# A decoder trunk on one core: x's second token tile is transposed inside the first weight chunk of the feature-form products

## The reference

```python
for i in range(DEPTH):                      # DEPTH = 2
    h = rms_norm(x, norm_mix_g[i])
    x = x + (moba_mixer(h, ...) if i == 0 else retention_mixer(h, ...))
    x = x + sqrelu_mlp(rms_norm(x, norm_mlp_g[i]), mlp_w1[i], mlp_w2[i])

def sqrelu_mlp(h, w1, w2):                  # w1 1024 x 4096, w2 4096 x 1024
    return jnp.square(jax.nn.relu(h @ w1)) @ w2
```

## Time and profile before

| | |
|---|---|
| median of 3 runs | 675.47 us (673.47 to 677.33) |
| the profiled execution | 677.14 us |
| its span, first to last instruction | 675.4 us |
| mean granted clock of TensorE in it | 0.995 |
| PE busy | 664.5 us, 98% |
| PEld busy | 559.1 us, 83% |
| DVE busy | 424.0 us, 63% |
| ACT busy | 330.9 us, 49% |
| POOL busy | 25.7 us, 4% |
| read from HBM | 121.52 MB, 181 GB/s over the span |

### The profile page before, as it was taken

How to read it: one execution, slowest core, us unless ns; L and a number is a source line. 1 busy time by engine, 2 the same in 40 slices (tenths; PEclk the granted TensorE clock), 3 DMA queues, 4 the chain that set the end, 5 groups by cost and what they waited for, 6 DMA issues and landing times.

```text
span 675.4 us, 8900 instructions
## 1 busy us (share of the span) xinstructions
PE 664.5 (98%) x3296; PEld 559.1 (83%) x3296; DVE 424.0 (63%) x466; ACT 330.9 (49%) x432; POOL 25.7 (4%) x35
## 2 busy tenths in 40 slices
PE   7998999999999999999999999999999999999998
PEld 5877888888888888888888888888888888888887
DVE  5877766777777444557985656554468777744441
ACT  6575764655555333436445554543365555533320
POOL 0341200000000000000000000000000000000000
PEclk7999999999999999999999999999999999999999
DMA  8954537476555655553666445536648665555600
GB/s 310 390 199 146 175 113 263 137 205 186 183 186 186 212 200 202 180 196 126 193 195 201 161 129 183 185 125 186 195 119 248 187 186 186 186 187 194 211 1 31
DMA packets 82077, 122.98 MB, mean 182 GB/s; under 512 B 2176, under 2 KB 43904, under 8 KB 82048
## 3 DMA queue, kind: packets, MB, share of 16 engines
q1 hardware_dynamic: 81472, 121.05, 55.0%
q0 software_dynamic: 288, 1.31, 0.5%
q10 hardware_dynamic: 288, 0.21, 0.1%
HBM read 121.52 MB, written 1.05 MB: 181 GB/s over the span
## 4 chain that ended last, share of the span: by engine, by line
PE 88%; issue 3%; DVE 3%; POOL 1%; ACT 1%; DMA 1%; SPq 1%; DVEq 0%; POOLq 0%; ACTq 0%
PE acc L552 22%; PE acc L483 17%; PE acc L485 17%; PE acc L484 17%; PE acc L555 11%; DVE lo L972 1%; DMA rope_in<-in_rope_in 1%; SPq L369 1%; ACT hi L737 1%; POOL rope_g L424 1%; PE scr L485 1%; PE scr L484 1%; PE scr L483 1%; PE scr L682 1%; PE scr L623 1%
## 5 line engine op out<-in xcount | busy, mean ns | idle before, releaser
L972 DVE TENSOR_TENSOR lo<-raw,hi 128x2048 fp32r<-128x2048 f32 x109 | 249.4, 2290 | 119.9 <-ACT hi L737 117.9
L737 ACT ACTIVATE hi<-raw 128x2048 fp32r<-128x2048 f32 x109 | 209.0, 1918 | 131.6 <-PE acc L485 128.6
L552 PE MATMUL acc<-h_both,hi 128*128 128x512 f32 x640 | 224.0, 396 | 0.0
L555 PE MATMUL acc<-h_both,lo 128*128 128x256 f32 x640 | 178.3, 279 | 0.0
L552 PEld LDWEIGHTS acc<-h_both,hi 128*128 128x128 f32 x640 | 120.1, 188 | 28.5
L555 PEld LDWEIGHTS acc<-h_both,lo 128*128 128x128 f32 x640 | 120.5, 188 | 0.0
L483 PE MATMUL acc<-hi,aT_hi 128*128 128x512 f32 x252 | 98.1, 389 | 0.0
L485 PE MATMUL acc<-hi,aT_lo 128*128 128x512 f32 x252 | 98.1, 389 | 0.0
L484 PE MATMUL acc<-lo,aT_hi 128*128 128x512 f32 x252 | 98.0, 389 | 0.0
L483 PE MATMUL acc<-hi,h_both 128*128 128x512 f32 x224 | 91.2, 407 | 2.5 <-DVE lo L1027 2.4
L485 PE MATMUL acc<-hi,h_both 128*128 128x512 f32 x224 | 88.5, 395 | 0.0
(11 more groups left out here) (124 smaller groups left out, 555.2 us busy)
## 6 DMA issues: line engine op xcount, KB each, us to landing
raw<-in_mlp_w SPq DMA_DIRECT2D x64, 1024.0 KB, 5.3
raw<-in_r_w_in SPq DMA_DIRECT2D x24, 1024.0 KB, 5.1
raw<-in_a_w_qkv SPq DMA_DIRECT2D x9, 1024.0 KB, 8.5
raw<-in_r_w_out SPq DMA_DIRECT2D x8, 1024.0 KB, 5.0
raw<-in_a_w_o SPq DMA_DIRECT2D x4, 1024.0 KB, 4.9
raw<-in_a_w_qkv SPq DMA_DIRECT2D x12, 256.0 KB, 7.3
x<-in_x SPq DMA_DIRECT2D x1, 1024.0 KB, 11.0
decay_sb<-in_decay POOLq DMA_DIRECT2D x1, 768.0 KB, 6.6
```

Source lines behind the costliest of these rows:

```text
L552: nc.tensor.matmul(bank, feat_view(hi, s)[:, kt, o * P:(o + 1) * P], h_both[:, kt, :, :].rearrange("p b t -> p (b t)"), start=kt == 0, sto ...
L555: m = nc.tensor.matmul(bank[:, 0:SEQ], feat_view(lo, s)[:, kt, o * P:(o + 1) * P], hT_hi[:, kt, :], start=False, stop=kt == KD - 1)
L737: nc.scalar.activation(hi[:, s, :], raw[:, s, :], ACT.Copy).then_inc(hi_ready, 1)
L972: nc.vector.tensor_tensor(lo[:, s, :], raw[:, s, :], hi[:, s, :].bitcast(F32), ALU.subtract).then_inc(lo_ready, 1)
```

## The change

TensorE's program alone is changed. The last four k tiles of x are no longer transposed in one call ahead of the first chunk. `first_wide_chunk` transposes tile 0, then runs the first chunk in quarters: half 0 with k tiles 0 to 3, then tile 1's transposes, half 1 with k tiles 0 to 3, half 0 with k tiles 4 to 7, half 1 with k tiles 4 to 7. It stands at the start of `mlp` and of the retention's q/k product, so at three places in the run. Each bank still gets its k tiles in ascending order.

```diff
+            def wide(bank, g, s, kt, o):
+                nc.tensor.matmul(bank, feat_view(hi, s)[:, kt, o * P:(o + 1) * P],
+                                 h_both[:, kt, :, :].rearrange("p b t -> p (b t)"), start=kt == 0, stop=False)
+                return nc.tensor.matmul(bank[:, 0:SEQ], feat_view(lo, s)[:, kt, o * P:(o + 1) * P],
+                                        hT_hi[:, kt, :], start=False, stop=kt == KD - 1)
+
-            def wide_feature_form(g, s, bank0, hT_need=None):
+            def wide_feature_form(g, s, bank0):
...
-            def transpose_x(norm, kts):
+            def transpose_x(norm, kts, tiles=range(TT)):
 
-                for t in range(TT):
+                for t in tiles:
...
+            def first_wide_chunk(g, norm, bank0):
+
+                last = range(4, KD)
+                transpose_x(norm, last, [0])
+                chunk_in(g, 0)
+                pe.wait_ge(acc_free, bank0 + 2)
+                for kts, o in ((range(4), 0), (range(4), 1), (last, 0), (last, 1)):
+                    for kt in kts:
+                        if o == 0:
+                            pe.wait_ge(hT_ready, 4 + 8 * norm + kt + 1)
+                        m = wide(acc[:, o, :], g, 0, kt, o)
+                    if kts == range(4) and o == 0:
+                        transpose_x(norm, last, [1])
+                m.then_inc(used, 1)
...
-            transpose_x(1, range(4, KD))
...
-                wide_feature_form(C_W1[layer] // 4, 0, B_W1[layer], hT_need=4 + 8 * norm)
+                first_wide_chunk(C_W1[layer] // 4, norm, B_W1[layer])
...
-            transpose_x(2, range(4, KD))
...
-            wide_feature_form(C_QK // 4, 0, B_QK, hT_need=4 + 8 * 2)
+            first_wide_chunk(C_QK // 4, 2, B_QK)
...
-            transpose_x(3, range(4, KD))
             mlp(1, 3)
```

More of the change, by code:

```diff
@@ L549, in wide_feature_form @@
                     for kt in range(KD):
[L550 to L556, removed]
+                        m = wide(bank, g, s, kt, o)
                 m.then_inc(used, 1)
-            def transpose_x(norm, kts):
-                for t in range(TT):
+            def transpose_x(norm, kts, tiles=range(TT)):
+                for t in tiles:
                     for kt in kts:
```

## The result

The changed kernel takes 676.25 us (median of 20, 673.98 to 677.93); the kernel before, in 20 executions on the same chip, 674.77 us (673.10 to 677.33). The ratio is 1.0021, with a 95% interval of 1.0011 to 1.0031: slower by 0.7 to 2.1 us, where 1.58 us less was forecast. The change of level is small, inside the 0.5% of the forecast, but its sign is clear of noise and is the other one.

The account below looks back on a forecast made before the run. TensorE's instruction stream was taken to bound the kernel; earlier starts less the transposes' cost gave 0.48, 0.62 and 0.48 us, 1.58 in all, so 675.47 became 673.9 us, range 671.9 to 676.3.

Parts of the forecast that it names:

- What bounds the kernel: TensorE's instruction stream plus its few stalls; stalls at three places of 0.86, 0.63 and 0.84 us, 2.33 in all.
- (a): At the three places, the first wide matmul starts 0.92, 1.06 and 0.92 us earlier, behind tile 0's transposes alone.
- (b): Four transposes inside the first chunk cost 0.35 us plus 0.09 for the dearer first period: 0.44, bounds 0.35 and 0.51.
- What would show it: Trace signs: no "DVE x" waits, no idle before third quarter or chunk 2, places shorter by 0.48, 0.62, 0.48 us.
- (c): x's tile 1 is ready before its moved transposes come up, with 0.99, 0.85 and 0.98 us of cover: no wait.
- (d): h's second half starts 0.85 to 0.99 us later; margins 0.46 and 0.30 us for h, 0.33 for bank 0: no cost.
- The sum: Over the whole run, 1.58 us less: span 675.6 us in place of 677.14 profiled, median 673.9 us in place of 675.47.
- 1 and 2: First: norm chain lags, half the gain lost, 674.7 us (0.10); second: chain waits for queued matmuls, 677.5 us (0.04).
- Rival 3: In the first chunk at each place the clock falls to half: 15.2 us more, 690.7 us, chance 0.01.
- the rule in the Trainium skill: Cycling through PSUM banks can idle TensorE so often that its clock swings; the changed chunk could run at half speed.
- Rival 5: No gain reaches the end because a load or another engine sets the pace later: 675.5 us, chance 0.05.
- The range: For the run time, 671.9 to 676.3 us: the forecast with some 2 us either side.

Follow-up runs that it names:

- m_only: Changed kernel with transposes still moved but the first chunk in bank order (bank 0 whole, then bank 1): 678.70 us, ratio 1.0053 to the kernel before.
- b_w8: Kernel before, with eight 512-column then eight 256-column matmuls per half in feature-form chunks behind the first: 675.92 us, ratio 1.0017.
- a35_w2: Changed kernel with transposes in groups of 3 and 5, and matmuls two and two in chunks behind the first: 672.54 us, ratio 0.9957 to the kernel before.
- w8: Changed kernel with eight 512-column then eight 256-column matmuls per half in chunks behind the first: 673.95 us, ratio 0.9984 to the kernel before.
- a_w8: Changed kernel with matmuls eight and eight behind the first chunk, run again for comparison on one chip: 673.99 us, ratio 0.9999 to the kernel before.
- kick1: Kernel before with 4, 1, 0 and 8 extra identity transposes ahead of feature-form chunks but the first, by ring place: 688.25 us, one execution.
- kick3: Kernel before with 5, 3, 4 and 2 extra identity transposes ahead of feature-form chunks, by ring place: 689.92 us, one execution.
- kick2: Kernel before with one 256-column, one 512-column, two 256-column or one 128-column extra matmul ahead of feature-form chunks but the first: 682.28 us, one execution.
- b_again: Kernel before, unchanged, run again for a second trace: 675.39 us, ratio 1.0002.
- o_only: Changed kernel with all eight transposes back ahead of the first chunk, only the quarter order kept: 675.34 us, ratio 1.0004 to the kernel before.
- a35_w8: Changed kernel, eight and eight behind the first chunk, transposes in groups of 3 and 5, first chunk's quarters grouped four and four: 674.00 us, ratio 0.9987.

## Why the prediction was wrong, point by point

- *What bounds the kernel.* Right: TensorE's stream, with 2.33 us of stalls.
- *(a), the first wide matmul.* Right: 0.92, 1.07 and 0.91 us earlier, for 0.92, 1.06 and 0.92.
- *(b), four transposes in the stream.* Right: 0.35 us, and 0.32 for the period behind them. Up to the start of chunk 2 the traces have 0.50, 0.44 and 0.48 us less than before, for the 0.48, 0.62 and 0.48 of "What would show it"; the second would be 0.65 had its two chunks the same pace on both sides. "So splitting the group costs nothing of its own" is right for the group, and wrong in what follows from it: the group changes the pace of what comes behind.
- *(c), x in time.* Right: no tile 1 group waits.
- *(d), what is late next.* Right: no wait of TensorE on h or on banks. The margins that were between 0.3 and 0.5 us held. The stall that m_only adds is the one that these rows give.
- *The sum.* The places gained 1.65 us where 1.58 was forecast. The step that failed is the one from the gain of the places to the time of the run, "less 1.58 it is 675.6": it puts at nothing what the change does to the 640 pairs behind, because "the same transposes, matmuls and waits are issued". I took a pair's duration for a constant ("The 0.35 of a pair comes from two whole chunks"), measured it in one product and used it for all. It has two values, 0.3467 and 0.3533 us, the trace of before had both (5.55 and 5.66 us per chunk), and which one a product gets is decided in its first chunk, which is exactly the spot that the change rearranges. The pairs at the long pace cost 2.56 and 4.27 us in the two traces of the changed kernel, 1.71 and 0.85 in those of the kernel before; by the shares above that is 2.8 us more on the mean, against the 1.65 gained. I read two chunks of the q/k product (11.17 us) and not the same two of the first MLP, which take 11.38.
- *Rivals.* 1 and 2 did not happen. Rival 3 had the right place and the wrong mechanism: the chunk's matmuls do get longer, but at full clock, by 2% instead of 100%, and for the whole product instead of one chunk. Of the rule in the Trainium skill, "TensorE: Matmul & The Clock Gate", section "A second HAM failure mode: psum-queue depth-cycling", no trace shows anything: the granted clock is 1.00 in all windows of the three places, and in both kernels from 20 us to the end of the last product. Rival 5, "Nothing reaches the end", is right in its effect, for another reason: what the places gained was lost inside TensorE's busy time, where "178.00 of 178.00 us" cannot show it.
- *The range* held the changed kernel's 676.25, at its very end, and by luck: it was wide for noise, not for this. The direction was wrong. A part of what I called spread of the runs (673.47 to 677.33) is this same pace: steps of 1.7 and 0.85 us on top of the start.

Not settled: why a given entry draws the one pace or the other. In all 24 products with the entry of the kernel before, the first step behind the transposes is 312 or 313 ns ahead of the short pace and 315 or 316 ahead of the long one. So a few ns go with the difference; whether they cause it is not shown, and behind the moved transposes the same step (314 ns) came with either pace. I have no run that shows what in TensorE holds the pattern.

## What to carry to other kernels

A stall removed on the busiest engine is worth its length only if the instructions behind it keep their pace; compare the pace of long streams (start to start, per chunk, per stage) between the two traces before believing a sum of stalls, and between stages of the trace of before to see whether it has more than one value. Where two alternating kinds of instruction settle into one of several repeating patterns, an order with one pattern only (here two and two instead of one and one) makes the gain of a removed stall visible; it can be slower than the better of the patterns (b_w8), and over the kernel before it showed a gain that stood clear of noise with all stalls gone (a35_w2), while that of eight and eight with stalls left did not repeat (w8, a_w8). And with two profiles of one execution each, look at more executions or an account per stage before reading their spans: here they had the wrong sign.

## What was not expected of the hardware

- Pairs of a 512- and a 256-column matmul in this number format, each with its weight load, run at 0.3467 or at 0.3533 us, at the full granted clock and without idle time, and hold that over 256 pairs (90 us) and over waits and loop branches. The shorter one has a second form, 230 and 117 ns again and again (q/k product of m_only).
- One to five transposes (kick1, kick3), or one matmul of another size (kick2), between two pairs can change the pace; the same interruption gives one or the other. Eight transposes, always behind a chunk at the short pace, left it short in 10 of 10 cases (kick1).
- The same matmuls two and two run at 5.573 us per chunk of 16 pairs and eight and eight at 5.587, each with one pace in every trace.
- The start of the kernel, up to the first place, took 117.5 to 119.9 us in traces of kernels that do not differ there. In four traces (before, b_again, o_only, a35_w8) the granted clock fell to 0.50 for 6.8 us from about 8.4 or 8.9 us on, and these four are the ones at 119.86 to 119.93; the others are at 117.50 to 119.08.
